# Differential attention in a two-layer encoder: the two softmax maps of a head joined before they meet V

## The chip, the core and the metric

The kernel runs on one core of a Trainium2 chip. The metric is the device time of one execution in microseconds (us), the median of three runs. TensorE multiplies and transposes, VectorE (DVE in the profile), ScalarE (ACT) and GpSimd (POOL) do the elementwise work, and SyncE (SP) issues the large transfers.

## What is computed

Two layers over 256 tokens of width 1024. Each layer projects the normalised input, runs four kinds of attention with four heads each, projects back, and adds a product-key feed-forward part (PEER). The change touches the attention alone. The kinds are A (latent attention), B (differential attention), C (chunked) and D (windowed, with sinks). B has two maps to a head:

```python
s = jnp.einsum('bqhmd,bkhmd->bmhqk', qb, k).astype(F32) * scale + bias[None, None].astype(F32)
p = masked_softmax(s, mask)
w = p[:, 0] - lam * p[:, 1]
return jnp.einsum('bhqk,bkhd->bqhd', w.astype(v.dtype), v)
```

The other kinds have one map: softmax of scaled scores plus a bias, times V. Scores are scaled by the head width to the power -1/2 and everything is float32.

## The kernel before, in words

Every engine has its own program, written out by hand, and the engines meet at semaphores that only count up. A layer goes: input projection in six chunks of weights (`project` on TensorE; each weight piece is split into a high part by ACT, line 1018, and a rest by POOL, line 566), query and key preparation, the attention loop, output projection, PEER. PEER takes most of the time: long uninterrupted runs of matmuls whose weights SP streams in.

**The attention loop** works on 15 groups of maps, `groups`, G0 to G14. A group is 512 columns of scores: four maps of 128 keys for the first 128 queries (G0 to G4), two maps of 256 keys for the second 128 queries (G5 to G14). In order of kinds: G0, G1 are B; G2 is C; G3 is D; G4 is A; G5 to G8 are B; G9, G10 are C; G11, G12 are D; G13, G14 are A. All engines step i from 0 to 17 in the same rhythm, each with its own share of a step:

- TensorE: `score(i)` (one matmul to a map into PSUM bank i % 3), `turn(i - 2)` (four 128x128 transposes of the probabilities into PSUM, line 601), `mix(i - 3)` (four matmuls with V, 64 columns each). A float32 matmul shows as two records in the trace. `mix` of the last four groups has five idle-filling transposes ahead of it (`keep_busy`).
- DVE: `biased(i)`: scale and add the bias from PSUM into `scores` (line 1423), then the negated maximum (line 1427); D has two small operations more (1431, 1433). Then `mixed(i - 3)`: reciprocal of the sums (1442), for B times minus lambda (1447), scale both maps' results (1450) and add them (1451); for the others one multiply (1454).
- ACT: `numerators(i)`: one Exp to a map with its sum (1081), then `turned(i - 1)`: copy of the turned probabilities out of PSUM (1089). In steps 7 to 10 it also makes the high part of one 512-wide piece of the output weights (`high_pieces`, line 1018), and POOL the rest of it (line 566).

`score(i)` waits until DVE has read the scores of group i - 3 (`sc_read`); `turn` waits for `probs_ready` and for the copy of group g - 3; `mix` waits for the copy and for `o_ready` of group g - 2. Each engine's stream is strictly in order, so whatever stands behind a waiting instruction waits too.

At the start of a layer DVE makes `gqm`, the per-row factors of the queries (line 1309, three small operations); ACT applies them when it copies the turned queries (line 982).

Of the kernel before, what the change touches and what calls it, by code (L numbers as in the profile page):

```python
# [15 lines left out]
P = 128  # L16
D = 1024
# [144 lines left out]
def build(nc, t, out):  # L162

    ctx = ExitStack()
    with ctx:
# [134 lines left out]
        def S(name):  # L300
# [12 lines left out]
         sc_done, sc_read, negmax_ready, probs_ready, pt_done, pt_ready, pv_done, o_ready, osq_ready, heads_ready,  # L313
# [7 lines left out]
            "sc_done sc_read negmax_ready probs_ready pt_done pt_ready pv_done o_ready osq_ready heads_ready "  # L321
# [6 lines left out]

        PER_LAYER = {}
        for count, which in (  # L330
                (1, "rms_ready gqm_ready cqt_done cqt_ready qka_ready prepped lists_ready best_shift "
                 "wexp_ready lists_t listt_ready acts_ready rs0_ready yt_cleared diag_ready rs_spread rs_kept"),
                (2, "kr_ready up_done up_copied lam_ready y_turned mean_ready root_ready "
                 "heads_ready heads0_ready yt_act yt_dve"),
                (3, "osq_ready k_evicted y_chunk"),
                (4, "hn_ready rs_used ht_done"),
                (7, "q_evicted"),
                (8, "xsq_done xt_done hsq_ready sq_used x_ready xf_ready"),
                (10, "tr_done"),
                (NB // OCT, "ones_ready"),  # L340
                (3, "picked"),
                (12, "h_ready"),
                (15, "sc_done sc_read negmax_ready probs_ready pt_done pt_ready pv_done o_ready"),
                (16, "ld_bias ld_wout ld_wq0 ld_wq1 ld_wq2 ld_wq3 qp_done qst_ready ks_done sraw_ready sq_kept wq_high "
                 "wq_rest gain_in"),
                (24, "fh_ready fl_ready"),
                (32, "ld_up"),
                (NG4, "hots_ready hota_act gate_done"),
                (NG4 + 2, "gated"),
                (64, "w_high w_rest w_used"),  # L350
                (NB, "gelu_used"),
                ((GT - 1) * NG4, "dist_ready"),
                (NK, "prod_done act_stored y_done"),
                (2 * NR, "gath_used"),
                (32 * NR // OCT, " ".join(f"gath_in{b}" for b in range(OCT))),
                (16 * (USES + NO), " ".join(f"nat_in{s}" for s in range(OCT))),
                (32, " ".join(f"spare_in{e}" for e in range(NE)))):
            for which_ in which.split():
                PER_LAYER[which_] = count

# [25 lines left out]
        NG = len(groups)  # L386

# [69 lines left out]
        with nc.Block() as block:  # L457
# [139 lines left out]
            def _(pe):  # L597
                for l in range(DEPTH):
# [133 lines left out]
                    def turn(g):  # L732
                        kind, tt, ms_ = groups[g]
                        pe.wait_ge(probs_ready, past[probs_ready] + g + 1)
                        if g == 1:
# [3 lines left out]
                        for i in range(4):  # L739
                            ins = tr(ps[:, 3 + g % 3, i * P:(i + 1) * P], probs[:, g % 3, i * P:(i + 1) * P])  # L740
                        ins.then_inc(pt_done, 1)

                    def mix(g):
# [6 lines left out]
                        for i in range(len(ms_)):  # L750
                            v = vcols(kind, ms_[i][3])
# [188 lines left out]
            def _(act):  # L940
                for l in range(DEPTH):
# [35 lines left out]
                    def evict_units(g, part_=None):  # L977
# [92 lines left out]
                    def numerators(g):  # L1070
# [9 lines left out]
                        for i in range(len(ms_)):  # L1080
                            ins = A(probs[:, b, i * n:(i + 1) * n], scores[:, b, i * n:(i + 1) * n], ACT.Exp,  # L1081
                                    bias=negmax[:, b4, i:i + 1], accum_out=rsum[:, b4, i:i + 1])
                        ins.then_inc(probs_ready, 1)

                    def turned(g):
# [3 lines left out]
                        A(pt[g % 2], ps[:, 3 + g % 3, :], ACT.Copy).then_inc(pt_ready, 1)  # L1089
# [143 lines left out]
            def _(dve):  # L1233
                ch = Chain(dve, dve_chain)
                for l in range(DEPTH):
# [72 lines left out]
                    for a, b, c in ((0, 4, 5), (4, 12, 3), (12, 16, 7)):  # L1308
                        ins = v.tensor_scalar(gqm[:, a:b], rowmask[:, a:b], gcol[:, c:c + 1], None, ALU.mult)  # L1309
# [96 lines left out]
                    def biased(g):  # L1406
# [8 lines left out]
                        if kind in "AB":  # L1415
                            step = m if kind == "A" else 2
                            bvs = [over(bias[:, 12 if kind == "A" else 4 + ms_[i][3], k0:], 1, step) for i in range(0, m, step)]
                        else:
                            step, h0 = m, BROW[kind] + ms_[0][3]
                            bvs = [bias[:, h0:h0 + m, k0:]]  # L1420
                        for i, bv in enumerate(bvs):
                            a, e = i * step * n, (i + 1) * step * n
# [13 lines left out]
                    def mixed(g):  # L1436
# [6 lines left out]
                        src = ps[:, 6 + g % 2, 0:m * HD]  # L1443
                        if kind == "B":
                            h0, w = 4 + ms_[0][3], m // 2
                            r2 = rinv[:, b, 0:m].rearrange("p (h m) -> p h m", m=2)
                            ch.step(v.tensor_scalar(r2[:, :, 1], r2[:, :, 1], lamt[:, 5:6], None, ALU.mult))
                            s4 = src.rearrange("p (h m d) -> p h m d", m=2, d=HD)
                            both = lists[:, 0, 0:m * HD].rearrange("p (h m d) -> p h m d", m=2, d=HD)
                            ch.step(v.tensor_tensor(both, s4, over(r2, 3, HD), ALU.mult))  # L1450
                            v.tensor_tensor(oall[:, tt, h0:h0 + w, :], both[:, :, 0, :], both[:, :, 1, :], ALU.add).then_inc(o_ready, 1)
                        else:
# [352 lines left out]
```

## Time and profile before

| | us |
|---|---|
| median of 3 runs (1591.59 to 1592.58) | 1592.3 |
| the profiled execution's own time | 1590.78 |
| its span in the trace | 1589.0 |
| attention loop, first layer (first bias step to last `mixed`) | 75.0 to 114.9 |
| busy: TensorE / DVE / ACT / POOL | 1565.9 / 1061.6 / 555.5 / 649.7 |

The profile is one execution. The chain of waits follows the work that ended last back from the end; for each group of instructions it gives the busy time and what ended the idle time before it. A "x12" behind a row is the number of records merged into it. The second layer repeats the first: the loop of layer 2 has the same steps 787.3 us later, so one is read for both.

### The profile page before, as it was taken

To read this page: it belongs to the slowest core of one execution; us is meant where nothing else is said; L and a number is where in the kernel's file an instruction comes from. 1 tells how busy PE (TensorE), PEld (TensorE's weight loads), DVE (VectorE), ACT (ScalarE), POOL (GpSimd) and SP (SyncE) were. 2 spreads that over 40 slices of the span, in tenths; PEclk is the share of its full clock that TensorE was granted. 3 is DMA by queue.
4 is the path that set the end of the run, shared out by engine and by line. 5 is a ranking of instruction groups with operands and counts; after the bars stand their busy time and mean duration, and the time that the engine had idled before them with its cause. 6 is when DMAs were issued, how large, how long until landed. Compare 5 with 4: busy or idle time off the path is not lost.

```text
span 1589.0 us, 32114 instructions
## 1 busy us (share of the span) xinstructions
PE 1565.9 (99%) x11432; PEld 1531.1 (96%) x11432; DVE 1061.6 (67%) x2523; ACT 555.5 (35%) x1538; POOL 649.7 (41%) x552
## 2 busy tenths in 40 slices
PE   7999999999999999999999999999999999999998
PEld 6888999999999999999978899999999999999998
DVE  4784899688888543444467848996888875434444
ACT  5686522655554000000067766126555530000000
POOL 6616604543555333222175175235333452332321
PEclk9999999999999999999999999999999999999999
DMA  9026288999999999999961252989999999999996
GB/s 364 5 107 265 94 326 329 335 410 409 409 409 410 408 410 410 410 406 408 404 229 66 96 238 95 361 300 379 409 409 409 409 409 409 410 407 405 408 405 255
DMA packets 141942, 525.76 MB, mean 331 GB/s; under 512 B 16160, under 2 KB 19744, under 8 KB 139424
## 3 DMA queue, kind: packets, MB, share of 16 engines
q1 hardware_dynamic: 86336, 322.57, 51.7%
q0 software_dynamic: 55520, 202.14, 32.4%
q8 instruction: 42, 0.69, 0.2%
q14 instruction: 44, 0.36, 0.1%
HBM read 523.60 MB, written 1.05 MB: 330 GB/s over the span
## 4 chain that ended last, share of the span: by engine, by line
PE 93%; DVE 3%; ACT 2%; issue 1%; POOL 1%; DMA 0%; SPq 0%; DVEq 0%; ACTq 0%
PE ps L604 90%; PE ps L601 2%; DMA x<-in_x 0%; DVE grid L1423 0%; DVE negmax L1427 0%; ACT grid L297 0%; ACT grid L982 0%; ACT wh L1018 0%; ACT grid L1081 0%; POOL wl L572 0%; ACT fhl L1004 0%; ACT grid L968 0%; DVE x L1485 0%; POOL wl L566 0%; DVE gqm L1309 0%
## 5 line engine op out<-in xcount | busy, mean ns | idle before, releaser
L604 PE MATMUL ps<-grid,ring 128*128 128x160 f32 (+1 forms) x3712 | 520.3, 299 | 0.0
L604 PE MATMUL ps<-grid,nat 128*128 128x160 f32 (+1 forms) x3712 | 520.3, 299 | 0.0
L604 PEld LDWEIGHTS ps<-grid,ring 128*128 128x128 f32 x3712 | 508.6, 190 | 0.0
L604 PEld LDWEIGHTS ps<-grid,nat 128*128 128x128 f32 x3712 | 508.6, 190 | 0.0
L1714 DVE SCALAR_TENSOR_TENSOR grid<-grid,amount 128x1024 f32<-128x1024 f32 x96 | 123.3, 1284 | 155.3 <-DMA grid<-in_peer_v,lists 155.2
L1714 DVE SCALAR_TENSOR_TENSOR grid<-gath_a,amount,grid 128x1024 f32<-128x1024 f32 x94 | 120.7, 1284 | 143.4 <-DMA gath_a<-in_peer_v,lists 143.2
L566 POOL TENSOR_TENSOR wl<-grid,wh 128x512 fp32r<-128x512 f32 (+2 forms) x128 | 142.2, 1142 | 144.3 <-ACT wh L1018 128.0
L586 POOL DMA_INDIRECT gath_a<-in_u_rows,lists x96 | 121.7, 1268 | 184.9 <-DVE dots L1683 132.2
L586 POOL DMA_INDIRECT gath_a<-in_peer_v,lists x96 | 103.1, 1074 | 203.1 <-DVE grid L1714 66.6
L586 POOL DMA_INDIRECT grid<-in_peer_v,lists x96 | 98.4, 1025 | 195.2 <-DVE grid L1714 70.8
L1018 ACT ACTIVATE wh<-grid 128x512 fp32r<-128x512 f32 (+2 forms) x128 | 67.8, 575 | 311.5 <-DMA grid<-in_w_in 273.4
L604 PE MATMUL ps<-grid 128*128 128x160 f32 (+5 forms) x1172 | 164.4, 298 | 0.0
L604 PEld LDWEIGHTS ps<-grid 128*128 128x128 f32 (+1 forms) x1172 | 155.6, 191 | 1.4
L586 POOL DMA_INDIRECT grid<-in_u_rows,lists x96 | 104.6, 1089 | 119.2 <-DVE dots L1683 109.1
L604 PE MATMUL ps<-wh,fhl 128*128 128x512 f32 (+2 forms) x512 | 124.3, 360 | 0.0
L1683 DVE CUSTOM_DVE_ANT_0 grid<-grid 128x1024 f32<-128x1024 f32 x96 | 116.3, 1221 | 10.5 <-DMA grid<-in_u_rows,lists 10.2
L1683 DVE CUSTOM_DVE_ANT_0 gath_a<-gath_a,grid 128x1024 f32<-128x1024 f32 x96 | 116.3, 1219 | 10.2 <-DMA gath_a<-in_u_rows,lists 10.0
L1182 ACT ACTIVATE ab<-ab,small,nwkt 128x128 f32<-128x128 f32 x240 | 101.1, 483 | 10.5 <-ACT ab L1179 10.0
L604 PEld LDWEIGHTS ps<-wh,fhl 128*128 128x128 f32 x512 | 88.9, 190 | 12.5
L993 ACT ACTIVATE grid<-ps 128x320 f32<-128x320 f32 x4 | 1.7, 437 | 279.5 <-PE ps L604 279.5
L1174 ACT ACTIVATE grid<-ps 128x160 f32<-128x160 f32 x160 | 46.8, 293 | 144.7 <-PE ps L604 104.9
L1179 ACT ACTIVATE ab<-iota,ikt 128x128 f32<-128x128 f32 x240 | 78.9, 392 | 46.0 <-PE ps L604 46.0
(202 smaller groups left out, 1737.5 us busy)
## 6 DMA issues: line engine op xcount, KB each, us to landing
nat<-in_peer_v SPq DMA_DIRECT2D x128, 512.0 KB, 11.4
ring<-in_peer_v SPq DMA_DIRECT2D x128, 512.0 KB, 11.6
nat<-in_peer_u SPq DMA_DIRECT2D x104, 512.0 KB, 7.6
ring<-in_peer_u SPq DMA_DIRECT2D x104, 512.0 KB, 7.5
grid<-in_peer_u SPq DMA_DIRECT2D x48, 512.0 KB, 6.1
grid<-in_peer_wq SPq DMA_DIRECT2D x8, 2048.0 KB, 10.3
grid<-in_w_out SPq DMA_DIRECT2D x2, 4096.0 KB, 12.4
grid<-in_w_in SPq DMA_DIRECT2D x3, 2048.0 KB, 15.9
```

Of the source, the lines that this page charges most:

```text
L566: nc.gpsimd.tensor_tensor(wl4[:, n % 4, 0:w], src, wh4[:, n % 4, 0:w].bitcast(F32), ALU.subtract).then_inc(w_rest, 1)
L586: nc.gpsimd.indirect_dma_start(gath[m % OCT], None, u_rows if m < NR else v_rows, bass.IndirectOffsetOnAxis(ap=lists[:, 3, NH + m % NR:NH ...
L601: return nc.tensor.transpose(dst, src, ident[:, :])
L604: return nc.tensor.matmul(dst, a, b, start=first, stop=last)
L993: A(yt[:, 2 * j:2 * j + 2, NS:], y_pair(j), ACT.Copy).then_inc(yt_act, 1)
L1018: A(wh4[:, n % 4, 0:w], src, ACT.Copy).then_inc(w_high, 1)
L1174: A(gelus[:, s % 4, :], ps[:, UBANKS[s % 4], 0:DT], ACT.Gelu_apprx_tanh).then_inc(act_stored, 1)
L1179: A(hota[:, s % 2, k, :], iota[:, :], ACT.Abs, bias=of_token(ikt, g, s, k), scale=-1.0).then_inc(dist_ready, 1)
L1182: ins = A(hota[:, s % 2, k, :], hota[:, s % 2, k, :], ACT.Relu, bias=of_token(wkt, g, s, k), scale=of_token(nwkt, g, s, k))
L1683: v.tensor_tensor_reduce(out=gath[b], in0=gath[b], in1=xs, scale=1.0, scalar=0.0, op0=ALU.mult, op1=ALU.add, accum_out=dots[:, n:n + 1]).t ...
L1714: v.scalar_tensor_tensor(out=acc, in0=gath[b], scalar=amount[:, n:n + 1], in1=acc, op0=ALU.mult, op1=ALU.add).then_inc(gath_used, 1)
```

## The change

The scaling of the scores moves into the queries (`gqm` is multiplied by it, and A's queries are scaled in ACT's copy). Bias and maximum become one instruction to a map, which writes the negated sum of score and bias and accumulates its minimum; Exp then runs with scale -1. The semaphore `sc_read` goes and `score` waits for `negmax_ready` instead.

For B a new DVE function `join(g)` stands at the head of step g + 2. With sums s1 and s2 it takes r = 1/s2 times minus lambda times s1, and adds r times the second map to the first, in place. Only the joined map is turned (two transposes instead of four), copied (256 columns instead of 512) and multiplied with V (two matmuls instead of four), and `mixed` only multiplies by 1/s1. `turn` of a B group waits for `joined`.

```diff
-                            pe.wait_ge(sc_read, past[sc_read] + g - 2)
+                            pe.wait_ge(negmax_ready, past[negmax_ready] + g - 2)
...
                         pe.wait_ge(probs_ready, past[probs_ready] + g + 1)
+                        if kind == "B":
+                            pe.wait_ge(joined, past[joined] + joins.index(g) + 1)
...
-                        for i in range(4):
-                            ins = tr(ps[:, 3 + g % 3, i * P:(i + 1) * P], probs[:, g % 3, i * P:(i + 1) * P])
+                        for i, c in enumerate(c for cs, _ in blocks(g) for c in cs):
+                            ins = tr(ps[:, 3 + g % 3, i * P:(i + 1) * P], probs[:, g % 3, c:c + P])
...
-                        for i in range(len(ms_)):
-                            v = vcols(kind, ms_[i][3])
+                        for i, (cs, head) in enumerate(blocks(g)):
+                            v = vcols(kind, head)
...
-                            ins = A(dst.rearrange("p u t -> p (u t)"), ps[0:AQK, bank, :], ACT.Copy)
+                            ins = A(dst.rearrange("p u t -> p (u t)"), ps[0:AQK, bank, :], ACT.Copy, scale=SCALE["A"] if g < 8 else 1.0)
...
-                                    bias=negmax[:, b4, i:i + 1], accum_out=rsum[:, b4, i:i + 1])
+                                    bias=negmax[:, b4, i:i + 1], scale=-1.0, accum_out=rsum[:, b4, i:i + 1])
...
-                        A(pt[g % 2], ps[:, 3 + g % 3, :], ACT.Copy).then_inc(pt_ready, 1)
+                        w = P * sum(len(cs) for cs, _ in blocks(g))
+                        A(pt[g % 2][:, 0:w], ps[:, 3 + g % 3, 0:w], ACT.Copy).then_inc(pt_ready, 1)
...
-                        ins = v.tensor_scalar(gqm[:, a:b], rowmask[:, a:b], gcol[:, c:c + 1], None, ALU.mult)
+                        ins = v.tensor_scalar(gqm[:, a:b], rowmask[:, a:b], gcol[:, c:c + 1], SCALE[kind], ALU.mult, ALU.mult)
...
-                            ins = v.scalar_tensor_tensor(out=dst[:, a:e].rearrange("p (h k) -> p h k", k=n), in0=src[:, a:e].rearrange("p (h k) -> p h k", k=n),
-                                                         scalar=SCALE[kind], in1=bv, op0=ALU.mult, op1=ALU.add)
-                        ins.then_inc(sc_read, 1)
-                        dve.wait_ge(sc_read, past[sc_read] + g + 1)
-                        red = v.tensor_reduce(negmax[:, b4, 0:m], dst.rearrange("p (h k) -> p h k", k=n), X, ALU.max, negate=True)
+                        for i, (_, _, _, j) in enumerate(ms_):
+                            row = 12 if kind == "A" else BROW[kind] + j
+                            red = v.tensor_tensor_reduce(out=dst[:, i * n:(i + 1) * n], in0=src[:, i * n:(i + 1) * n], in1=bias[:, row, k0:], scale=-1.0,
+                                                         scalar=3e38, op0=ALU.add, op1=ALU.min, accum_out=negmax[:, b4, i:i + 1])
...
+                    def join(g):
+                        kind, tt, ms_ = groups[g]
+                        n, b, b3, m = P * (tt + 1), g % 4, g % 3, len(ms_)
+                        dve.wait_ge(probs_ready, past[probs_ready] + g + 1)
                         ch.step(v.reciprocal(rinv[:, b, 0:m], rsum[:, b, 0:m]))
...
+                        ch.step(v.scalar_tensor_tensor(out=r2[:, :, 1], in0=r2[:, :, 1], scalar=lamt[:, 5:6], in1=s2[:, :, 0], op0=ALU.mult, op1=ALU.mult))
+                        for i in range(0, m, 2):
+                            one, two = (probs[:, b3, c * n:(c + 1) * n] for c in (i, i + 1))
+                            ins = v.scalar_tensor_tensor(out=one, in0=two, scalar=rinv[:, b, i + 1:i + 2], in1=one, op0=ALU.mult, op1=ALU.add)
+                        ins.then_inc(joined, 1)
...
                     for i in range(NG + 3):
+                        if i - 2 in joins:
+                            join(i - 2)
                         if i < NG:
                             biased(i)
```

On DVE, step 9 of the loop (`biased(9)`, `mixed(6)`) reads before (`grid` holds scores, bias, probabilities and results; `ps` is PSUM):

```order
L1423 SCALAR_TENSOR_TENSOR grid<-ps,grid 128x512 [waits probs_ready,sc_done]
L1427 TENSOR_REDUCE negmax<-grid 128x2 [waits sc_read]
L1442 RECIPROCAL rinv<-rsum 128x2 [waits pv_done]
L1447 TENSOR_SCALAR rinv<-rinv,lamt 128x1 [waits dve_chain]
L1450 TENSOR_TENSOR lists<-ps,rinv 128x128 [waits dve_chain]
L1451 TENSOR_TENSOR grid<-lists 128x64 [waits dve_chain]
```

The same step in the changed kernel is `join(7)`, `biased(9)`, `mixed(6)`:

```order
L1457 RECIPROCAL rinv<-rsum 128x2 [waits probs_ready]
L1459 SCALAR_TENSOR_TENSOR rinv<-rinv,lamt,rsum 128x1 [waits dve_chain]
L1462 SCALAR_TENSOR_TENSOR grid<-grid,rinv 128x256 [waits dve_chain]
L1429 ISA grid,negmax<-ps,grid 128x256 [waits probs_ready,sc_done]
L1429 ISA negmax 128x1
L1429 ISA grid,negmax<-ps,grid 128x256
L1429 ISA negmax 128x1
L1450 TENSOR_TENSOR grid<-ps,rinv 128x64 [waits pv_done]
```

What DVE did for B behind `mix` it now does mostly ahead of `turn`; the bias step is two pairs of instruction and accumulator read; and `mixed` is a single multiply.

On TensorE, `turn(8)`, `mix(7)`, `score(11)` (step 10 into 11) before:

```order
L601 MATMUL ps<-ident,grid 128x128 [waits pt_ready,probs_ready]
L601 MATMUL ps<-ident,grid 128x128 x3
L604 MATMUL ps<-grid 128x64 [waits pt_ready,o_ready]
L604 MATMUL ps<-grid 128x64 x3
L604 MATMUL ps<-grid 128x256 [waits sc_read]
L604 MATMUL ps<-grid 128x256
```

and in the changed kernel:

```order
L610 MATMUL ps<-ident,grid 128x128 [waits pt_ready,joined,probs_ready]
L610 MATMUL ps<-ident,grid 128x128
L613 MATMUL ps<-grid 128x64 [waits pt_ready,o_ready]
L613 MATMUL ps<-grid 128x64
L613 MATMUL ps<-grid 128x256 [waits negmax_ready]
L613 MATMUL ps<-grid 128x256
```

Two transposes and two matmuls are gone, and the transposes wait for one semaphore more.

## Rows read from the trace of the kernel before

**Rows 1.** Chain of waits in the first loop: start, us, what
```profile
93.37 0.70 DVE grid L1423
...
95.50 0.78 issue
...
107.16 1.20 PE ps L601 x9
108.36 0.84 PE ps L604 x8
```

**Rows 2.** Busy time by stretch: length, engines, granted TensorE clock (PEclk), DMA
```profile
84.00:88.00 4.00, 4.00 (x34) 3.85 (x34) 3.76 (x11) 4.00 (x19) 0.00 (x0) 1.00 0.99 426
...
93.00:107.00 14.00, 13.79 (x98) 12.19 (x96) 12.96 (x35) 11.71 (x36) 5.09 (x4) 1.00 0.00 1
```

**Rows 3.** Timeline of TensorE in the loop: start, us, line, operation
```profile
88.78 0.60 PE L601 MATMUL ps<-ident,grid 128*128 128x128 f32 x4
...
93.17 0.60 PE L601 MATMUL ps<-ident,grid 128*128 128x128 f32 x4
93.60 1.92 PE L604 MATMUL ps<-grid 128*128 128x64 f32 x12
...
97.56 0.60 PE L601 MATMUL ps<-ident,grid 128*128 128x128 f32 x4
...
111.85 1.00 PE L604 MATMUL ps<-grid 128*128 128x64 f32 x8
```

**Rows 4.** Timeline of DVE in the loop
```profile
95.46 0.89 DVE L1451 TENSOR_TENSOR grid<-lists 128x64 f32<-128x64 f32 x1
96.28 0.68 DVE L1423 SCALAR_TENSOR_TENSOR grid<-ps,grid 128x512 f32<-128x512 f32 x1
...
97.59 0.15 DVE L1442 RECIPROCAL rinv<-rsum 128x2 f32<-128x2 f32 x1
97.78 0.22 DVE L1447 TENSOR_SCALAR rinv<-rinv,lamt 128x1 f32<-128x1 f32 x1
98.03 0.29 DVE L1450 TENSOR_TENSOR lists<-ps,rinv 128x128 f32<-128x128 f32 x1
98.36 0.23 DVE L1451 TENSOR_TENSOR grid<-lists 128x64 f32<-128x64 f32 x1
98.50 0.68 DVE L1423 SCALAR_TENSOR_TENSOR grid<-ps,grid 128x512 f32<-128x512 f32 x1
...
112.89 0.17 DVE L1442 RECIPROCAL rinv<-rsum 128x2 f32<-128x2 f32 x1 [1.07 <-PE ps L604]
```

**Rows 5.** Timeline of POOL: the first of four output-weight pieces in the loop
```profile
95.00 1.27 POOL L566 TENSOR_TENSOR wl<-grid,wh 128x512 fp32r<-128x512 f32 x1 [18.38 <-ACT wh L1018]
```

**Rows 6.** Timeline of ACT: copy of turned probabilities, then a high piece
```profile
93.80 0.60 ACT L1089 ACTIVATE grid<-ps 128x512 f32<-128x512 f32 x1
94.30 0.62 ACT L1018 ACTIVATE wh<-grid 128x512 fp32r<-128x512 f32 x1
```

**Rows 7.** ACT by form, 60 to 119 us: busy us, mean ns
```profile
L1081 ACT ACTIVATE grid<-grid,negmax 128x256 f32<-128x256 f32 x20 | 10.0, 498 | 1.6 <-DVE negmax L1427 1.3
...
L1081 ACT ACTIVATE grid<-grid,negmax 128x128 f32<-128x128 f32 x20 | 7.8, 398 | 1.8 <-DVE negmax L1427 1.8
```

**Rows 8.** Timeline of DVE: two narrow bias steps, then the fused instruction in PEER
```profile
75.00 0.76 DVE L1423 SCALAR_TENSOR_TENSOR grid<-ps,grid 128x256 f32<-128x256 f32 x2 [3.34 <-PE ps L604]
...
253.31 1.22 DVE L1683 CUSTOM_DVE_ANT_0 gath_a<-gath_a,grid 128x1024 f32<-128x1024 f32 x1
254.46 0.08 DVE L1683 DVE_READ_ACCUMULATOR2_ANT dots<- 128x1 f32 x1
```

**Rows 9.** The page: the costliest instruction with a per-partition scalar and two inputs
```profile
L1714 DVE SCALAR_TENSOR_TENSOR grid<-grid,amount 128x1024 f32<-128x1024 f32 x96 | 123.3, 1284 | 155.3 <-DMA grid<-in_peer_v,lists 155.2
```

**Rows 10.** Timelines of DVE and POOL at the making of `gqm`
```profile
22.79 1.33 DVE L1309 TENSOR_SCALAR gqm<-rowmask,small 128x8 f32<-128x8 f32 x1
...
22.81 1.29 POOL L566 TENSOR_TENSOR wl<-grid,wh 128x512 fp32r<-128x512 f32 x1
```

More of the change, by code:

```diff
@@ L326, in build @@
             "y_done y_chunk diag_ready rs_spread rs_kept sq_kept lam_ready gain_in picked gath_used acts_ready yt_act yt_dve yt_cleared y_turned mean_ready root_ready rs0_ready heads0_ready").split())
[L329 to L359, printed above, removed]
         def earlier(l):
@@ L386, in build, with blocks @@
         NG = len(groups)
+        joins = [g for g in range(NG) if groups[g][0] == "B"]
+        def blocks(g):
+            kind, tt, ms_ = groups[g]
+            step = 2 if kind == "B" else 1
+            return [([(i * (tt + 1) + kb) * P for kb in range(tt + 1)], ms_[i][3]) for i in range(0, len(ms_), step)]
+        PER_LAYER = {}
+        for count, which in (
+                (1, "rms_ready gqm_ready cqt_done cqt_ready qka_ready prepped lists_ready best_shift "
+                 "wexp_ready lists_t listt_ready acts_ready rs0_ready yt_cleared diag_ready rs_spread rs_kept"),
+                (2, "kr_ready up_done up_copied lam_ready y_turned mean_ready root_ready "
+                 "heads_ready heads0_ready yt_act yt_dve"),
+                (3, "osq_ready k_evicted y_chunk"),
+                (4, "hn_ready rs_used ht_done"),
+                (7, "q_evicted"),
+                (sum(g[0] == "B" for g in groups), "joined"),
+                (8, "xsq_done xt_done hsq_ready sq_used x_ready xf_ready"),
+                (10, "tr_done"),
+                (NB // OCT, "ones_ready"),
+                (3, "picked"),
+                (12, "h_ready"),
+                (15, "sc_done negmax_ready probs_ready pt_done pt_ready pv_done o_ready"),
+                (16, "ld_bias ld_wout ld_wq0 ld_wq1 ld_wq2 ld_wq3 qp_done qst_ready ks_done sraw_ready sq_kept wq_high "
+                 "wq_rest gain_in"),
+                (24, "fh_ready fl_ready"),
+                (32, "ld_up"),
+                (NG4, "hots_ready hota_act gate_done"),
+                (NG4 + 2, "gated"),
+                (64, "w_high w_rest w_used"),
+                (NB, "gelu_used"),
+                ((GT - 1) * NG4, "dist_ready"),
+                (NK, "prod_done act_stored y_done"),
+                (2 * NR, "gath_used"),
+                (32 * NR // OCT, " ".join(f"gath_in{b}" for b in range(OCT))),
+                (16 * (USES + NO), " ".join(f"nat_in{s}" for s in range(OCT))),
+                (32, " ".join(f"spare_in{e}" for e in range(NE)))):
+            for which_ in which.split():
+                PER_LAYER[which_] = count
         class Chain:
@@ L1441, in mixed @@
                             ch.step(v.tensor_tensor(rsum[:, b, 0:m], rsum[:, b, 0:m], sinke[:, b, 0:m], ALU.add))
-                        ch.step(v.reciprocal(rinv[:, b, 0:m], rsum[:, b, 0:m]))
[L1443 to L1452, printed above, removed]
-                            h0 = HROW[kind] + ms_[0][3]
-                            v.tensor_tensor(oall[:, tt, h0:h0 + m, :], src.rearrange("p (h d) -> p h d", d=HD),
-                                            over(rinv[:, b, 0:m], 2, HD), ALU.mult).then_inc(o_ready, 1)
@@ new lines, in mixed @@
+                        if kind == "B":
+                            h0, m, by = 4 + ms_[0][3], m // 2, rinv[:, b, 0:m].rearrange("p (h m) -> p h m", m=2)[:, :, 0]
+                        else:
+                            h0, by = HROW[kind] + ms_[0][3], rinv[:, b, 0:m]
+                            ch.step(v.reciprocal(by, rsum[:, b, 0:m]))
+                        v.tensor_tensor(oall[:, tt, h0:h0 + m, :], ps[:, 6 + g % 2, 0:m * HD].rearrange("p (h d) -> p h d", d=HD),
+                                        over(by, 2, HD), ALU.mult).then_inc(o_ready, 1)
```

16 lines of the change are left out of this document (5 added, 11 removed).

## The prediction, on record before the run

> **What bounds the kernel now.** I read the chain of waits first, then the busy time by stretch, then the timelines of the attention loop engine by engine. The change touches only that loop, 40 us of each layer, and the loop ends in the output projection, which waits for it; so what the loop gains or loses arrives at the end, twice, since the second layer repeats the first. PEER behind it is TensorE's own work and only shifts.
>
> Within the loop the bound moves. From 84 to 88 us ACT and TensorE are both busy for 4.00 of 4.00 us [rows 2]: one step is four Exps and a copy on ACT, and on TensorE four transposes, four matmuls with V and a score. TensorE repeats at 2.20 us a step: 88.78 to 93.17 is two steps, and 93.17 to 97.56 two more [rows 3]. Its parts: transposes 0.43 (93.17 to 93.60), then 1.76 for `mix` and `score`; `mix` alone is 0.84 [rows 1], so `score` is 0.92. But at 93.37 the chain changes to DVE [rows 1], and it stays there until turn(12) at 107.16. TensorE still looks busy to 97.56 because it runs ahead; from turn(8) at 97.56 to turn(12) at 107.16 it needs 9.60 us for four steps of 2.20. In B's steps DVE does bias and maximum in 1.31 (96.28 to 97.59) and `mixed` in 0.91 (to 98.50), 2.22 together. Step 8 took 2.91, and here is the reason: line 1451 lasted 0.89 us instead of 0.23 [rows 4], since POOL worked from 95.00 to 96.27 [rows 5]. That instruction has both inputs in SBUF; it got through 0.08 us behind POOL's end, as if it had started 0.15 before it. The chain calls this "issue" [rows 1]. The other instructions of `mixed`, one input in PSUM or only a few elements, do not wait.
>
> **The change part by part, in one layer.**
>
> *Bias and maximum.* The fused instruction is in PEER already: 1.22 us for 1024 columns, the accumulator read starts 1.15 behind it, and takes 0.08 [rows 8]. Two bias instructions of 256 columns from PSUM take 0.76, one 0.41 and the next 0.35 later; 512 columns take 0.68, so a column is 1.05 ns. So 256 fused columns are 0.34 to the next instruction, two maps 0.68 in place of 1.31. The upper bound is 0.49 each, the narrow bias instruction and a read that isn't covered: 0.98. I take 0.68, since the row for the same instruction is nearest. With either, DVE stops being the bound of the second half.
>
> *Steps 0 to 5.* The first two B groups save two copies' width on ACT, 0.20 each (128 columns more cost an Exp 0.10 [rows 7]), and DVE now waits for the Exps in join(0) and join(1) with the bias of G2 and G3 queued behind, which ACT needs next. I set the two against each other: turn(4) stays at 88.78, give or take 0.4.
>
> *The new wait.* Before, TensorE needed only the Exps of a group, which lay ready. Now turn(g) needs join(g), and that stands on DVE behind mixed(g - 2), which waits for mix(g - 2), which stands on TensorE behind turn(g - 1). That is a ring. Its parts: 0.20 from mix to DVE (111.85 + 0.84 to 112.89 [rows 3, 4]); reciprocal 0.19 to the next (97.59 to 97.78); a small instruction with a per-partition scalar 0.25 (97.78 to 98.03); the join itself 0.48, which is 1284 ns for 1024 columns [rows 9] less 768 columns; 0.05 back to TensorE. So join to turn is 0.97.
> - turn(5) = 88.78 + 0.44 + 0.84 + 0.20 + mixed(3) 0.72 (add, reciprocal, multiply of 256 columns) + 0.97 = 91.95, against 90.97 before: **0.98 lost**.
> - turn(5) to turn(6): 0.22 + 0.84 + 0.20 + mixed(4) 0.53 + 0.97 = 2.76.
> - turn(6) to turn(7) to turn(8): 0.22 + 0.42 + 0.20 + 0.14 + 0.97 = 1.95 each. So turn(8) at 98.61, against 97.56: 1.05 lost so far.
> - From turn(8) TensorE is the bound alone: 0.22 + 0.42 + 0.92 = 1.56, then 0.44 + 0.42 + 0.92 = 1.78, then 2.20 twice; 7.74 in place of 9.60, **1.86 won**. The tail behind turn(12) is unchanged.
>
> Net, with nobody in the way, 0.81 us a layer, 1.6 us in all.
>
> *The join and POOL.* The join has both inputs in SBUF, as line 1451 has. In steps 7 to 10 ACT makes a weight piece right after `turned`, and POOL follows it. Count both from T, the start of turn(6). POOL: two transposes 0.22, 0.19 to the copy (93.17 + 0.44 to 93.80 [rows 3, 6]), a copy of 256 columns 0.30 (0.50 less 0.20), and 0.70 from high piece to POOL (94.30 to 95.00 [rows 5, 6]): T + 1.41. The large instruction of join(7): 0.22 + 0.42 + 0.20 + 0.14 + 0.19 + 0.25 = T + 1.42. A tie, and the same tie again for join(8) against the next piece, as the ring and the piece both hang on `turn`. The loser waits. If it is the join it starts 0.15 before POOL's end, at T + 2.53, 1.1 late, on the ring. If it is POOL, nothing: its pieces are needed only behind the loop. Who wins a tie? Two DVE instructions at `gqm` start 20 ns ahead of POOL and still last 1.33 us, to POOL's end [rows 10]. So a join must lead by more than that, and I have it 0.01 behind. I take the collision: two of 1.1 us a layer. The page SBUF — State Buffer of the Trainium skill (Who interferes with whom) says that two SBUF inputs contend with a GpSimd instruction reading SBUF, and that issue order decides who blocks; by its word alone a join 20 ns ahead would go free. The rows on `gqm` speak against that for starts as close as these.
>
> *Edits at nothing.* `gqm` with a second operation and the scale in A's copy: same instructions, same lengths. If the new `gqm` no longer waited for POOL it could give back at most some 1 us in all. `score` waiting for `negmax_ready` instead of `sc_read`: three groups of slack. The second small join instruction also has two SBUF inputs, but ends before POOL starts. ACT's narrower copies in steps 6 to 9: not on the ring.
>
> **Sum.** Two layers of -0.81 + 2.2 = +1.4: **+2.8 us**. The profiled execution took 1590.78 and would take 1593.6; the median of the runs lies 1.5 higher, so 1595.1. A difference under 0.2%, 3.2 us, is about what a measurement of this kernel cannot tell from no change, so this counts as no change.
>
> **Rivals.**
> - *The join slips ahead of POOL* (chance 0.3). Then the sum is -1.6: 1590.7. For it: the difference is 0.01 us out of 1.4, and a record's start is not the moment of the lock. Against it: every error that makes the ring longer (an uncovered read, a costlier join) puts the join behind. Its own range is 1589.2 to 1592.
> - *One join of two meets a piece, or start and end cancel* (0.12): about 1592.5.
> - *TensorE's clock falls* (0.08), the case that ends clearly slower. TensorE was busy 13.79 of 14 us here at granted clock 1.00 [rows 2], the 2.4 GHz level. With both collisions turn(5) to turn(9) takes 2.76 + 3.05 + 3.05 + 1.56 = 10.4 us for 1.98 + 3 x 1.56 = 6.7 us of work, 64%. If the clock halves then, TensorE's 7.74 us behind turn(8) become up to 15.5; half of that loss, 3.9 a layer, gives 1595.1 + 7.8 = 1602.9. It decides from the point where the clock leaves 1.00 in that stretch. Against it: no idle gap in this reckoning is longer than 1.5 us (3.05 less 1.56). The page TensorE: Matmul & The Clock Gate of the Trainium skill (Part 1) has the clock follow how busy the array was; no stretch of this trace shows a fall.
>
> **How the numbers follow.** Collision 0.50, ahead of POOL 0.30, mixed 0.12, clock 0.08. The unknown prices (join 0.42 to 0.48 on four rings, start of the loop 0.4, the fused instruction) move each case by about 1.2 us. The forecast's own range is 1593.6 to 1596.7. The range over all reaches down through the second case and leaves out the clock: 1589.4 to 1597.2. Slower by over 3.2 us: a third of the collision case, 0.17, and the clock, 0.08: 0.25. Faster by over 3.2: 0.10, the far end of the second case and a `gqm` that no longer waits. The rest, 0.65, is no change.
>
> **What would show it.** Right: turn(5) near 92, turn(8) near 100.8, turn(12) near 108.5; the join of G7 and G8 lasting about 1.6 us and ending 0.08 behind POOL's piece, those of G5 and G6 0.48; the bias step 0.68; granted clock 1.00. Wrong: all joins at 0.48 (then turn(12) near 106.4 and the second case holds), a bias step above 1 us, or turn(5) at 91, which would mean that the ring doesn't bind. I would be wrong altogether if PEER's length changed.

## The result, and the profile after

The changed kernel takes **1598.5 us** (median of six executions, 1596.7 to 1600.4); the kernel before, run beside it, 1591.9. The ratio is 1.0043, with a 95% interval of 1.0032 to 1.0054: it is slower by 6.6 us, outside the range that was given (up to 1597.2), and by more than a measurement blurs. The profiled execution took 1596.68 us with a span of 1594.9, against 1590.78 and 1589.0; it was the fastest of the six.

Where `turn` starts, in us, from the timelines of TensorE. The prediction's column counts from the same origin as before; the trace of after lies 0.08 later at turn(0).

| | before | predicted | after | after, layer 2, less turn(0) | before, layer 2, less turn(0) |
|---|---|---|---|---|---|
| turn(0) | 79.39 | | 79.47 | 0 | 0 |
| turn(1) | 82.01 | | 83.25 | 3.79 | 2.62 |
| turn(4) | 88.78 | 88.78 | 88.79 | 10.96 | 9.38 |
| turn(5) | 90.97 | 91.95 | 92.05 | 14.21 | 11.57 |
| turn(8) | 97.56 | 100.8 | 101.06 | 23.23 | 18.16 |
| turn(12) | 107.16 | 108.5 | 108.99 | 31.16 | 27.76 |

In layer 1 the loop goes as the prediction has it, to half a microsecond. Layer 2 is not its copy: up to turn(12) layer 1 takes 29.52 us and layer 2 takes 31.16. The loops give 1.75 + 3.40 of the 5.9 us by which the span grew. The rest, 0.7, lies between turn(12) of layer 1 and turn(0) of layer 2. That stretch takes 759.6 us before and 760.3 after, and 759.6 to 760.8 in the traces of the experiments, without order in what they changed. So it looks like the difference of one execution from another; no run here singles it out.

DVE's timeline at the two joins that meet POOL, and behind them the bias step, two pairs of the fused instruction and its accumulator read:

```profile
96.35 1.54 DVE L1462 SCALAR_TENSOR_TENSOR grid<-grid,rinv 128x256 f32<-128x256 f32 x1
97.81 0.41 DVE L1429 CUSTOM_DVE_ANT_0 grid<-ps,grid 128x256 f32<-128x256 f32 x1
98.16 0.07 DVE L1429 DVE_READ_ACCUMULATOR2_ANT negmax<- 128x1 f32 x1
98.16 0.41 DVE L1429 CUSTOM_DVE_ANT_0 grid<-ps,grid 128x256 f32<-128x256 f32 x1
98.50 0.08 DVE L1429 DVE_READ_ACCUMULATOR2_ANT negmax<- 128x1 f32 x1
...
99.42 1.54 DVE L1462 SCALAR_TENSOR_TENSOR grid<-grid,rinv 128x256 f32<-128x256 f32 x1
```

POOL's timeline in the same stretch:

```profile
96.34 1.26 POOL L575 TENSOR_TENSOR wl<-grid,wh 128x512 fp32r<-128x512 f32 x1 [19.64 <-ACT wh L1029]
99.42 1.26 POOL L575 TENSOR_TENSOR wl<-grid,wh 128x512 fp32r<-128x512 f32 x1 [1.81 <-ACT wh L1029]
```

The tie is there: join 96.35 against piece 96.34, then 99.42 against 99.42. Both joins last 1.54 us instead of the 0.48 of G5 and G6, and DVE's next instruction starts 0.21 behind POOL's end (the join itself is recorded to 0.29 behind it). Layer 2 has the same two, 1.55 and 1.54. The fused instruction is followed 0.35 later by its read and 0.34 to 0.35 by the next one, the read lying beside it: a bias step of 0.69, where [rows 4] had 1.31.

TensorE's timeline in layer 1, with the idle time before an instruction in brackets:

```profile
83.25 0.41 PE L610 MATMUL ps<-ident,grid 128*128 128x128 f32 x2 [2.51 <-DVE grid L1462]
83.50 1.50 PE L613 MATMUL ps<-grid 128*128 128x64 f32 x12
84.84 0.60 PE L610 MATMUL ps<-ident,grid 128*128 128x128 f32 x4
...
92.05 0.41 PE L610 MATMUL ps<-ident,grid 128*128 128x128 f32 x2 [0.90 <-ACT grid L1092]
...
97.99 0.41 PE L610 MATMUL ps<-ident,grid 128*128 128x128 f32 x2 [1.35 <-ACT grid L1092]
...
101.06 0.41 PE L610 MATMUL ps<-ident,grid 128*128 128x128 f32 x2 [1.35 <-ACT grid L1092]
```

and at the same place of layer 2:

```profile
873.07 0.41 PE L610 MATMUL ps<-ident,grid 128*128 128x128 f32 x2 [2.51 <-DVE grid L1462]
...
875.55 1.06 PE L610 MATMUL ps<-ident,grid 128*128 128x128 f32 x4
```

The two rows in the ring name ACT as releaser, and ACT had long been done: the wait is for several semaphores, and it is the join (it ends 0.1 earlier) that opens it. The line that matters is the first: ahead of turn(1) TensorE is idle for 2.51 us, which the prediction never spoke of. Before the change the same line read:

```profile
82.01 0.66 PE L601 MATMUL ps<-ident,grid 128*128 128x128 f32 x4 [1.13 <-ACT grid L1081]
```

In layer 1 the four transposes of turn(2) then take 0.60; in layer 2, after an idle time of the same length, 1.06. The busy time by stretch says why (its columns are those of [rows 2]; the granted clock stands behind the engines):

```profile
873.00:875.00 2.00, 1.94 (x12) 1.97 (x13) 1.33 (x11) 1.69 (x9) 0.00 (x0) 0.66 1.02 442
875.00:876.50 1.50, 1.50 (x9) 1.50 (x9) 0.70 (x7) 0.98 (x6) 0.00 (x0) 0.50 1.06 459
876.50:878.00 1.50, 1.50 (x9) 1.39 (x9) 0.52 (x5) 1.35 (x6) 0.00 (x0) 0.81 0.81 350
```

TensorE's clock is at its lower level, 1.2 GHz, in part of the first stretch, all of the second and part of the third. That is the difference between the layers.

So three theories to tell apart. **A**: the result is the sum of the collisions (about 1.06 us each, four of them), the ring, and a clock that falls because TensorE waits 2.51 us ahead of turn(1). **B**: the clock falls because of the many gaps of up to 1.35 us in the ring, as my rival had it. **C**: the join or the fused instruction is itself dear.

### The profile page after: what moved, and what is told of

It is laid out like the page before. It is cut to its first block, busy times and chain, and to the rows that moved or that the text cites. A ratio compares the mean times of both kernels' runs of the same rounds, so it can differ in the third digit from the quotient of the medians.

```text
span 1594.9 us, 32072 instructions
## 1 busy us (share of the span) xinstructions
PE 1560.8 (98%) x11360; PEld 1524.0 (96%) x11360; DVE 1052.0 (66%) x2623; ACT 552.8 (35%) x1538; POOL 646.4 (41%) x552
## 4 chain that ended last, share of the span: by engine, by line
PE 91%; ACT 3%; DMA 2%; DVE 2%; issue 1%; POOL 1%; SPq 0%; DVEq 0%; ACTq 0%
PE ps L613 89%; PE ps L610 2%; DMA grid<-in_peer_v,lists 1%; DMA grid<-in_w_in 1%; ACT grid L1092 0%; ACT grid L993 0%; ACT grid L297 0%; ACT wh L1029 0%; ACT fhl L1015 0%; POOL wl L581 0%; ACT grid L979 0%; POOL wl L575 0%; DVE x L1495 0%; DVE fhl L1304 0%; DVE gqm L1321 0%
## 5 line engine op out<-in xcount | busy, mean ns | idle before, releaser
L595 POOL DMA_INDIRECT gath_a<-in_u_rows,lists x96 | 118.4, 1233 | 188.5 <-DVE dots L1693 137.4
L595 POOL DMA_INDIRECT grid<-in_peer_v,lists x96 | 102.0, 1063 | 194.2 <-DMA nat<-in_peer_v 65.7
L613 PE MATMUL ps<-grid 128*128 128x160 f32 (+5 forms) x1124 | 160.1, 300 | 0.0
L613 PEld LDWEIGHTS ps<-grid 128*128 128x128 f32 (+1 forms) x1124 | 151.5, 192 | 1.3
```

The lines of the kernel that those rows point to most:

```text
L595: nc.gpsimd.indirect_dma_start(gath[m % OCT], None, u_rows if m < NR else v_rows, bass.IndirectOffsetOnAxis(ap=lists[:, 3, NH + m % NR:NH ...
L613: return nc.tensor.matmul(dst, a, b, start=first, stop=last)
```

## The experiments

Each was timed against the kernel before on the same chip, and its line gives both medians. Where two experiments of different chips are compared, it is by their distances from the kernel before. Behind a ratio stands its 95% interval; 0.001 of it is 1.6 us.

### Filling the idle time, and moving the collisions away

Sixteen idle-filling transposes go ahead of turn(1), behind the work that TensorE has anyway, so that its idle time shrinks and nothing else moves:

```diff
                     def turn(g):
                         kind, tt, ms_ = groups[g]
+                        if g == 1:
+                            keep_busy(6, 16)
```

> The changed kernel with 16 idle-filling transposes on TensorE ahead of turn(1), nothing else. In the changed kernel TensorE sits idle for 2.51 us there in both layers, and in layer 2 the granted clock fell to 0.50 for 3.4 us right after it, which made turn(1) to turn(3) 4.97 us in place of 3.34 in layer 1. Theory (the clock after the wait for join(1) costs 1.8 us each time it falls, in one or both layers, and explains why runs spread from 1596.7 to 1600.4): granted clock 1.00 in the loops of both layers, turn(12) of layer 2 exactly as far from its loop's start as in layer 1, median 1.8 to 3.6 us below the changed kernel's 1598.5, near 1595.5, and a narrower spread. Rival (the slower layer 2 comes from something else, such as transfers): the time stays near 1598.5.

Measured: 1595.9 us (1594.5 to 1598.6) against 1591.5, ratio 1.0031 [1.0021, 1.0042]. TensorE in layer 2:

```profile
869.69 1.91 PE L610 MATMUL ps<-ident 128*128 128x128 f32 x16
872.37 0.41 PE L610 MATMUL ps<-ident,grid 128*128 128x128 f32 x2 [0.77 <-issue]
...
873.95 0.60 PE L610 MATMUL ps<-ident,grid 128*128 128x128 f32 x4
```

Idle time is down to 0.77, turn(2) takes 0.60, the clock is 1.00 throughout both loops, and the two layers take 29.63 and 29.52 us from turn(0) to turn(12), though the gaps in the ring are all still there. With more work on TensorE the kernel is 4.4 us above the one before instead of 6.6. That is A, not B. The medians alone would not settle it, since the two intervals overlap (3.3 to 6.7 us here, 5.1 to 8.6 for the changed kernel); the traces do. Not as expected: the spread is no narrower (1594.5 to 1598.6, against 1596.7 to 1600.4).

The second leaves the idle time and takes the collisions away: ACT and POOL make their weight pieces two steps later, when all joins are done.

```diff
-                        if NG0 + 1 < i < NG0 + 6:
-                            high_pieces(NPI + i - NG0 - 2, NPI + i - NG0 - 1)
+                        if NG0 + 3 < i < NG0 + 8:
+                            high_pieces(NPI + i - NG0 - 4, NPI + i - NG0 - 3)
```

> The changed kernel with the four output-weight pieces of ACT and POOL moved from steps 7 to 10 to steps 9 to 12. Theory (the joins of G7 and G8 wait 1.06 us each for a POOL piece and carry it on the ring): all joins of 256 columns last 0.48, turn(6) to turn(7) and turn(7) to turn(8) take 2.0 each in place of 3.07, and each layer wins 2.1 us, 4.3 in all, so about 1594.2. Rival (the ring is held by something else, the wait is hidden): under 1 us won.

Measured: 1594.4 us (1591.8 to 1596.6) against 1591.5, ratio 1.0018 [1.0009, 1.0027]. DVE at the joins of G7 and G8:

```profile
98.30 0.48 DVE L1462 SCALAR_TENSOR_TENSOR grid<-grid,rinv 128x256 f32<-128x256 f32 x1
...
100.31 0.48 DVE L1462 SCALAR_TENSOR_TENSOR grid<-grid,rinv 128x256 f32<-128x256 f32 x1
```

The joins take 0.48 and follow at 2.01 us, where they followed at 3.07. By the distances the kernel is 3.7 us faster than the changed one, where 4.3 was expected. And the clock fell in this profiled execution in both layers, which the busy time by stretch shows:

```profile
85.00:88.40 3.40, 3.40 (x15) 3.13 (x14) 1.23 (x9) 3.40 (x17) 0.00 (x0) 0.50 1.06 455
873.50:880.30 6.80, 6.80 (x29) 6.33 (x30) 2.74 (x21) 4.80 (x23) 0.00 (x0) 0.50 1.04 448
```

The same program kept its clock in other executions. Its eleven times sort themselves by the mean granted clock of the execution: 1591.8 to 1592.8 us at 0.999 and 1.000 (three), 1593.8 to 1594.4 at 0.997 (three), 1595.7 to 1596.6 at 0.996 (five). So the falls of the clock go with 4 us between executions of one program, and without them this version is about where the kernel before is.

The third does both:

> Both of the former: filled idle time ahead of turn(1), and the pieces moved to steps 9 to 12. If the two costs are all that stood between the changed kernel and the sum without them, each layer's loop is 0.3 to 0.8 us shorter than before and the time is 1590.5 to 1592, equal to the kernel before. If it stays above 1594, a cost outside the loop is open.

Measured: 1591.3 us (1590.2 to 1593.1) against 1591.5, ratio 1.000 [0.9991, 1.0009]. TensorE in layer 1:

```profile
93.00 0.41 PE L610 MATMUL ps<-ident,grid 128*128 128x128 f32 x2 [0.90 <-ACT grid L1094]
...
97.99 0.41 PE L610 MATMUL ps<-ident,grid 128*128 128x128 f32 x2 [0.29 <-ACT grid L1094]
...
100.01 0.41 PE L610 MATMUL ps<-ident,grid 128*128 128x128 f32 x2 [0.29 <-ACT grid L1094]
```

Between this and the first lie only the collisions: 4.6 us for four, and the two turns of each layer that paid for them are 1.06 us shorter each. What is left, join and ring together with the fused bias, is worth nothing in sum. The profiled executions of the two kernels also give the price of the falls: turn(0) to turn(12) takes 27.51 and 27.41 us here, 29.07 and 30.71 in the one before, so 1.6 us for the fall in layer 1 (the stretch of 3.40 us above) and 3.3 us for the one in layer 2 (the stretch of 6.80).

### The fused bias and maximum alone

The changed kernel without any join: `mixed`, `turn` and `mix` as before the change, the scale in the queries and the fused instruction kept.

```diff
-            step = 2 if kind == "B" else 1
+            step = 1
...
-                        if i - 2 in joins:
-                            join(i - 2)
```

> The half of the change that touches the bias: scale moved into the queries, one fused instruction to a map for bias and maximum; no join, four transposes and both maps times V as before, and the old mixed for B. Theory (DVE bounds the kernel before from turn(8) to turn(12), 9.60 us, and the fused step takes 0.68 in place of 1.31): TensorE bounds the whole loop, turn(8) to turn(12) 8.8, about 0.8 us won a layer, 1590.7. Rival (everything the change loses comes with the fused instruction): slower than before.

Measured: 1589.9 us (1588.2 to 1591.5) against 1591.5, ratio 0.9989 [0.998, 0.9998]; and once more on another chip:

> The fused bias and maximum without any join once more, on the same chip as the earlier join, to compare the two: about 1589.9 (1.6 below the kernel before). If the early join is worth what the ring theory says it is some 3 us faster than this one; if the join brings nothing beyond the fused instruction the two are equal.

Measured: 1590.6 us (1588.6 to 1592.2) against 1591.6, ratio 0.9995 [0.9986, 1.0004], which is not clear of no change. In both traces TensorE now repeats at 2.20 us through all of B's steps; layer 1 of the first:

```profile
95.84 0.60 PE L609 MATMUL ps<-ident,grid 128*128 128x128 f32 x4
...
98.04 0.60 PE L609 MATMUL ps<-ident,grid 128*128 128x128 f32 x4
```

The 9.60 us from turn(8) to turn(12) are 8.79. The fused instruction gains 0.8 us a layer and is then hidden behind TensorE; line 1451 still meets POOL here (0.82 to 1.15 us instead of 0.23), on a DVE that now has time for it. Theory C falls for this half.

### The clock again, without added work

Filling adds work. The opposite test takes away what lengthens the wait: G0 and G1 are not joined, everything else of the change stays.

```diff
-        joins = [g for g in range(NG) if groups[g][0] == "B"]
+        joins = [g for g in range(NG0, NG) if groups[g][0] == "B"]
...
-            step = 2 if kind == "B" else 1
+            step = 2 if g in joins else 1
```

> The changed kernel, but the first two B groups (G0, G1) are not joined; they are turned, multiplied and mixed as before the change. The joins of G5 to G8 stay, collisions with POOL and all. If the idle stretch ahead of turn(1) comes from join(1) and the clock falls because of it, that stretch is back at 1.13 us, the granted clock is 1.00 in both loops, turn(8) to turn(12) is unchanged, and the time is that of the kernel with filled idle time, about 1595.9. If the clock fell for another reason (the gaps of 1.35 us in the ring, say), the time stays near 1598 with spread and some run shows a clock of 0.5 in the loop.

Measured: 1594.7 us (1593.9 to 1597.3) against 1591.6, ratio 1.002 [1.0011, 1.0029], 1.2 below the number I gave. TensorE in layer 2, and the stretch in which the clock had fallen:

```profile
870.68 0.66 PE L610 MATMUL ps<-ident,grid 128*128 128x128 f32 x4 [1.13 <-ACT grid L1092]
```

```profile
873.00:875.00 2.00, 2.00 (x17) 1.95 (x17) 1.74 (x12) 2.00 (x11) 0.00 (x0) 1.00 1.14 492
```

The wait is 1.13 us as before the change, and the clock holds in both loops (1.00 from 78 to 110 and from 866 to 900 us); turn(0) to turn(12) takes 29.68 and 29.59 us. In layer 1, where the changed kernel's clock held as well, it took 29.52: joining the first two groups neither won nor cost time in the loop, it only opened the idle stretch.

The other executions bear this out. The mean granted clock of a whole execution is on record for each: it is under 0.999 only in the three kernels with the wait of 2.51 us, in two of six executions of the changed kernel (0.998 and 0.997, its two slowest), in eight of eleven of the second experiment, and in two of five of the next one below. In the 81 executions of the other experiments it is 0.999 or 1.000. Of the six loops with that wait that have a trace the clock fell in four, of the 18 without it in none.

### Who wins the tie

First with POOL delayed a little: it clears 16 unused columns ahead of each of the four pieces.

```diff
+                        if NPI <= n < NPI + 4:
+                            nc.gpsimd.memset(plate[:, 4 * l + n - NPI, :], 0.0)
                         nc.gpsimd.tensor_tensor(wl4[:, n % 4, 0:w], src,
```

> The changed kernel, but POOL clears 16 unused columns ahead of each of the four output-weight pieces that it makes inside the loop, so that the piece itself starts some 0.1 to 0.2 us later. If who starts first decides, the joins of G7 and G8 now lead and last 0.48 us, the ring runs at about 2.0 us a step instead of 3.07, it is POOL's piece that is stretched (about 1.7 us), and the time falls by 4 x 1.06 us to about 1594.3 (with the clock fall still in it). If POOL wins over DVE whoever comes first, or if the join is simply slow next to any POOL work, the joins stay at 1.5 us or more and the time stays near 1598.5.

Measured: 1597.1 us (1596.4 to 1598.6) against 1591.6, ratio 1.0035 [1.0022, 1.0049]. Neither of the two outcomes: the strip moved POOL by 0.07 us only, and of four joins one came free. (The clock fell here too, in layer 2, as it did in the changed kernel.) DVE in layer 2:

```profile
887.25 1.59 DVE L1465 SCALAR_TENSOR_TENSOR grid<-grid,rinv 128x256 f32<-128x256 f32 x1
...
890.38 0.48 DVE L1465 SCALAR_TENSOR_TENSOR grid<-grid,rinv 128x256 f32<-128x256 f32 x1
```

and POOL:

```profile
887.31 1.26 POOL L578 TENSOR_TENSOR wl<-grid,wh 128x512 fp32r<-128x512 f32 x1
...
890.42 1.57 POOL L578 TENSOR_TENSOR wl<-grid,wh 128x512 fp32r<-128x512 f32 x1
```

All four joins are recorded 0.04 to 0.06 ahead of POOL. Three still lost, one of them at 0.06; one at 0.04 won, and then it was POOL that took 0.31 longer. So POOL has no fixed precedence, and records this close do not tell who will win. The Trainium skill, SBUF — State Buffer (Who interferes with whom), says that issue order decides. The traces agree where the records are 0.18 us apart (the next run); at 0.06 or less they do not show the order. With four strips, 0.07 each, on the kernel that joins only G5 to G8:

> The kernel with joins for G5 to G8 only, and ahead of each of the four weight pieces POOL clears four strips of 16 unused columns (0.07 us each by the last run with one strip), so that the large instruction of join(7) and join(8) leads POOL's piece by about 0.25 us instead of the 0.05 us at which it still lost three times in four. If the start decides and 0.05 us is only too close to call, all joins last 0.48 us, turn(6) to turn(8) takes 4.0 us instead of 6.1, POOL's piece takes about 0.2 us more, and the time is 4 x 1.06 us below the same kernel without strips: about 1590.5. If POOL takes precedence whoever is first, the joins last 1.5 us or more and the time stays near 1594.7.

Measured: 1591.1 us (1590.1 to 1592.1) against 1591.1, ratio 1.000 [0.9991, 1.0009]; the number given was 1590.5. DVE in layer 1, then POOL:

```profile
96.26 0.48 DVE L1476 SCALAR_TENSOR_TENSOR grid<-grid,rinv 128x256 f32<-128x256 f32 x1
```

```profile
96.44 1.43 POOL L579 TENSOR_TENSOR wl<-grid,wh 128x512 fp32r<-128x512 f32 x1
98.26 0.25 POOL L578 MEMSET plate<- 128x16 f32 x4 [0.38 <-ACT wh L1033]
98.46 1.43 POOL L579 TENSOR_TENSOR wl<-grid,wh 128x512 fp32r<-128x512 f32 x1
```

With a lead of 0.18 us all four joins take 0.48, and the pieces 1.43 instead of 1.27. Against the same kernel without strips, a delay of 0.2 us on the engine that nobody waits for gives 3.2 us, where 4 x 1.06 was expected; in the two traces the loops are 2.2 and 2.1 us shorter.

### The ring

If the join must not stand behind `mixed` (which waits for `mix`, which stands behind the last `turn`), it can go one step earlier, behind the bias step of the next group; there it waits for its Exps alone. With the pieces two steps later, and G0 and G1 unjoined:

```diff
                     for i in range(NG + 3):
-                        if i - 2 in joins:
-                            join(i - 2)
                         if i < NG:
                             biased(i)
+                        if i - 1 in joins:
+                            join(i - 1)
```

> As the last, and in addition the joins of G5 to G8 stand one step earlier on DVE, behind the bias step of the next group and ahead of the mixing, so that turn no longer waits for mix through DVE; and the weight pieces are made two steps later. If the ring through mix is what cost time in steps 5 to 8, turn(5) comes 2.2 us behind turn(4), the next three steps take 1.9 to 2.0 us each, and turn(12) is about 15.9 us behind turn(4) where it was 18.4 before the change and 18.2 with later pieces: about 1586.7 in all. If DVE is instead held up waiting for the Exps of the same group, steps 5 to 8 take 2.5 us or more and the time is near 1590 or above.

Measured: **1587.0 us** (1586.1 to 1587.5) against 1591.6, ratio 0.9968 [0.9957, 0.998]. It beats both kernels. TensorE in layer 1:

```profile
90.76 0.38 PE L610 MATMUL ps<-ident,grid 128*128 128x128 f32 x2
...
92.78 0.41 PE L610 MATMUL ps<-ident,grid 128*128 128x128 f32 x2
...
94.86 0.41 PE L610 MATMUL ps<-ident,grid 128*128 128x128 f32 x2 [0.36 <-issue]
...
96.53 0.41 PE L610 MATMUL ps<-ident,grid 128*128 128x128 f32 x2
```

Turn(5) comes 2.19 behind turn(4) (88.57) where it came 3.26 behind, and the next steps take 2.02, 2.08 and 1.67. Turn(4) to turn(12) takes 15.89 us, against 18.38 before the change and 20.20 after it. Here the smaller TensorE work of the joined heads pays at last: 3.6 us more than the fused instruction alone, timed on the same chip. So the join is not dear in itself either, and theory C falls for the other half too. Last, the same with the pieces where the change had them:

> The best kernel so far (1587.0: joins one step earlier, weight pieces two steps later) with the weight pieces back where the change had them, to tell how much of its gain needs the later pieces. The first piece would start 1.41 us behind turn(6), which is 0.08 us ahead of the large instruction of join(7): that join is held for 1.06 us, and join(8) may or may not meet the second piece. One collision a layer gives about 1589, two 1591. If DVE has room in those steps (it waits for nobody there, so the ring theory says it has none), the time stays at 1587.

Measured: 1589.0 us (1588.0 to 1590.3) against 1591.1, ratio 0.9988 [0.9979, 0.9997]. DVE:

```profile
94.72 1.47 DVE L1472 SCALAR_TENSOR_TENSOR grid<-grid,rinv 128x256 f32<-128x256 f32 x1
...
97.38 0.48 DVE L1472 SCALAR_TENSOR_TENSOR grid<-grid,rinv 128x256 f32<-128x256 f32 x1
```

POOL's pieces start at 94.65 and 97.72: the first join is 0.07 behind and is held, the second leads by 0.34 and goes free. One collision a layer, 2 us in all, as worked out beforehand. From the kernel with late joins this one differs in nothing but the place of the join, and it is 5.3 us faster (2.1 below the kernel before instead of 3.1 above): the ring, and one collision a layer less.

## Why the prediction was wrong

**The step that failed is "Steps 0 to 5".** It said: DVE now waits for the Exps in join(0) and join(1), G0 and G1 save width elsewhere, "I set the two against each other: turn(4) stays at 88.78". As a balance of time that is right to 0.1 us. Turn(1) comes 1.16 later behind turn(0) (3.78 us instead of 2.62), because join(1) is put between the Exps of G1 and its turn, as the chain of waits shows; turn(2) and turn(3) win it back (1.59 and 1.75 us behind the turn ahead of them, instead of 2.37 and 2.20):

```profile
82.07 0.19 DVE rinv L1457
...
82.28 0.23 DVE rinv L1459
...
82.81 0.35 DVE grid L1462
83.16 0.09 issue
```

But a balance says nothing of the hole in the middle. TensorE's wait ahead of turn(1) grew from 1.13 to 2.51 us, and behind a wait of that length the clock fell: in one layer of the profiled execution, in both of the one with later pieces, in one of the one with a single strip, and in none where the wait was 1.13 or 0.77. In the profiled executions the growth of 5.9 us is, rounded, the 2.8 of the sum, 1.6 for the one fall of the clock, 0.7 for loops that are each 0.36 longer than I had them, and the 0.7 between the loops. The fall is the term that carries the result over the end of the range: 1598.5 less 1.6 is 1596.9, and with the wait filled or the two joins left out the time is 1595.9 or 1594.7, all inside it.

How much of the 6.6 us the clock costs in the median is not shown as sharply. Filling the wait brought 2.2 us, leaving the two joins out 3.4, but four of the six executions, the median's neighbours among them, have a mean clock of 0.999. The profiled one has 0.999 too, with its one fall of 3.4 us, and a second would take another 0.001 off; so I estimate one fall at most for each of the four, 1.6 us. What the edits brought beyond that has no cause on record.

**The rival of the falling clock was right in kind and wrong in place.** I put it behind turn(5), on low activity with gaps under 1.5 us, and gave it 0.08, writing that "no idle gap in this reckoning is longer than 1.5 us". The reckoning had no row for the longest gap, since I had costed those steps as one number. In the ring, with its gaps of 0.70 to 1.40 us, the clock stayed at 1.00 in every trace. Nor is it so that "no stretch of this trace shows a fall". At the end of the trace of before TensorE's last instruction ends at 1584.5, and the clock is at its lower level from 1587.3 on, where nothing waits for it any more:

```profile
1587.30:1588.90 1.60, 0.00 (x0) 0.00 (x0) 0.00 (x0) 0.00 (x0) 0.00 (x0) 0.50 0.47 173
```

The price was too high as well: 7.8 us, where a fall cost 1.6 us and the longest 3.3.

**The collision: right.** A tie at T + 1.42 against T + 1.41 was on record, with 1.1 us for the loser and DVE as loser. Measured 96.35 against 96.34, 1.06 us more for each of four joins, and 4.6 or 3.2 us less in all when they are taken away in two different ways. That it came out at all is partly luck, as I had it: two sums that differ by 0.01 us of 1.4. The list of signs did not fit the sum: a join that starts 0.15 before POOL's end and lasts 0.48 ends 0.33 behind it, not 0.08; measured 0.29. And "only a few elements, do not wait" was too wide. In the changed kernel an instruction of two columns with both inputs in SBUF took 1.12 us beside POOL, instead of 0.16:

```profile
105.58 1.12 DVE L1436 TENSOR_TENSOR sinke<-negmax,small 128x2 f32<-128x2 f32 x1
```

```profile
105.41 1.27 POOL L575 TENSOR_TENSOR wl<-grid,wh 128x512 fp32r<-128x512 f32 x1 [1.64 <-ACT wh L1029]
```

**The ring: right.** turn(5) 91.95, measured 92.05; turn(5) to turn(6) 2.76, measured 2.87; 1.95 + 1.1 a step, measured 3.07; without collision 1.95, measured 2.01; behind turn(8) 1.56 and 1.78, measured 1.56 and 1.77, then 2.40 where I had 2.20. From turn(4) to turn(12) that is 20.20 us measured against 19.77, 0.43 too little.

**The fused instruction and the edits at nothing: right.** The bias step is 0.69 for 0.68, and the three instructions of `gqm` take 2.90 us together where they took 2.84 (2.64 and 2.85 in layer 2), so they still wait for POOL.

With the clock holding, the change costs 3.1 us where G0 and G1 stay unjoined and 4.4 where the wait is filled, against the +2.8 of the sum. Of the 1.3 between these two I know no cause, their loops being equal to 0.1 us; their intervals overlap (1.8 to 4.6 and 3.3 to 6.7 us), so it may be nothing. It stays open, as do the 0.7 us between the loops. How often the clock falls in the changed kernel is known only from the mean clocks: only one of its executions has a trace.

## What to carry to other kernels

When an edit delays one engine's start of a step and shortens later ones, write down the longest idle stretch of TensorE that comes of it, not only the balance: here a wait that grew from 1.13 to 2.51 us and was won back in time still cost 1.6 us in the traced execution through the clock, and up to 4.9 in that of the kernel with later pieces. An instruction that reads two SBUF operands and stands on the critical ring must not start in step with POOL's work; 0.2 us of delay on the idle engine, or the same work two steps later, was worth 3 to 5 us. And new work that is put between producer and consumer belongs as early in the engine's order as its own inputs allow: the same join one step earlier was worth 5.3 us, one collision a layer included, and turned a loss into a gain.

## What I had not expected of the hardware

- The granted clock went to 0.50 behind an idle time of 2.51 us, in one layer of an execution and not in the other with an equal idle time. A program with that wait kept its clock in some executions and lost 4 us in others. The waits of 1.13 us ahead of turn(1), and of up to 1.40 us in the ring, never had a fall behind them.
- A DVE instruction recorded 0.06 us ahead of POOL's can still be the one that waits (0.04 to 0.06 ahead lost three times of four); 0.18 was enough for it to win four times out of four. When DVE wins, POOL's instruction is recorded longer by 0.16 to 0.31 us.
- Filling idle time with unneeded transposes made the kernel faster: 16 of them, 1.91 us of TensorE's time in each layer, for 2.2 us less in all.
